# Seven block products in both feed-forward blocks, down sets 3 and 2 in turn

## The chip, the cores and the metric

One NeuronCore of a Trainium2 chip runs the whole program. The metric is the device time of one execution in microseconds. Engines as the profile names them: PE is TensorE, DVE VectorE, ACT ScalarE, POOL GpSimd, SP the engine that issues all DMAs here.

## The reference

Two transformer-like blocks on 1024 tokens of width 1024, all in float32. Only the feed-forward parts matter here:

```python
def swiglu(h, w_gate, w_up, w_down):                     # block 1, D_FF = 2816
    return (jax.nn.silu(h @ w_gate) * (h @ w_up)) @ w_down
...
h = h + swiglu(rmsnorm(h, norm_ffn[i]), w_gate[i], w_up[i], w_down[i])
...
h = rmsnorm_2(x, g_ffn[i])                               # block 2, D_FF_2 = 4096
x = x + jnp.square(jax.nn.relu(h @ w_ffn_up[i])) @ w_ffn_down[i]
```

## The kernel before

Each engine has one program, a chain of generators (`tensor`, `vector`, `scalar`, `gpsimd`, `sync`, L4056 to L4133), written out stage by stage: output projection of block 1 (`mix_`), FFN1 (`ffn_`), the latent projections (`z_`) and so on, `mix2_`, FFN2 (`ffn2_`), and a last gated stage (`ple_`). Every engine runs its list strictly in that order; semaphores (`Signal`) join them. A PSUM bank holds 128 x 512 floats; `tile_of` takes the next bank of a group and waits until its last tenant was read.

Precision: every operand is split into a high half (ScalarE copies into fp32r) and a low half (VectorE subtracts), and each product is three matmuls of 128 x 128 by 128 x 512: high by high, high by low, low by high.

FFN1 before (`ffn_blocks`, L1675 on) goes through the 22 row tiles of the hidden layer in chunks of 2 and then 4. For a pair of tiles it computes gate and up with `dense` (two tiles, two token halves, eight channel steps), multiplies by the norm's factor while draining (VectorE), applies Silu (ScalarE), multiplies, and splits the result into `f_hi` (ScalarE) and `f_lo` (POOL). Each chunk then has its down products, added to `hT` by VectorE. The weights stream through three slots of `wt1`. The last chunk's drains are followed tile by tile by the next stage's operand: ScalarE's high half and two squares, VectorE's low half and two sums (L1763 to L1771, L1823 to L1828).

FFN2 before uses seven block products in place of eight. A block of the up weights (8 channel tiles x 256 columns) and x are both seen as 2 x 2; `Sevens.add` makes four sums of quarters, `seven_products` runs seven products of depth 4 (84 matmuls) into three banks x, y, z in which the sums chain up (`BANK_OF`), ScalarE keeps the running bank three times (`kept`), and VectorE adds it to y and z. The first block is plain (96 matmuls), because the sums of x come late. VectorE also makes four differences of the f tiles, and SP stores seven tiles of 256 KB a block to `f_scratch`.

The down product (`Sets`, L565 on) has seven sets, each over all groups of depth 4, a piece being one set and group: 4 x 4 x 3 = 48 matmuls. Order 0, 3, 2, 6, 4, 1, 5. Weights and f come from DRAM, 1 MiB each a piece; a piece of sets 3, 2, 6 and 4 needs a sum of weights, made by VectorE in one of three `w_second` buffers. Set 3's sums are stored to DRAM and read by set 2, set 2's by set 6. Loads are issued four pieces ahead (`RINGS`), h is read back in quarters, and the set ends are added to it. SP's order in a piece is: wait for the piece, `second_free` (L627 to L631: the store that reads the buffer must have landed), loads, read-back, and the store of the sum two pieces on:

```python
        for i in range(LAST + 1):
            if i + RINGS <= LAST:
                q.wait_ge(*T.of("down2", i))
                dn.second_free(q, i + RINGS)
                dn.load_weights(q, i + RINGS)
                dn.load_moving(q, i + RINGS)
...
            if i + 2 <= LAST:
                dn.keep(q, i + 2)
```

## Time and profile before

| | us |
|---|---|
| median of 3 runs | 2906.4 (2905.8 to 2911.11) |
| the profiled execution | 2911.59 |
| its span, first to last instruction | 2909.8 |
| TensorE busy | 2765.3 (15516 matmuls) |
| VectorE, ScalarE, POOL busy | 1604.2, 864.7, 356.0 |
| FFN1 | 322.6 to 1050.1 |
| FFN2, up and down | 2110.0 to 2763.1 |

All times inside the execution are us from the start of its span. Matmuls overlap their neighbours, so busy times and lengths of one matmul say little; starts and the idle times before an instruction do. A number in square brackets behind a row is the idle time of that engine before it, with what ended it.

### The profile page before, as it was taken

To read this page: it belongs to the slowest core of one execution; us is meant where nothing else is said; L and a number is where in the kernel's file an instruction comes from. 1 tells how busy PE (TensorE), PEld (TensorE's weight loads), DVE (VectorE), ACT (ScalarE), POOL (GpSimd) and SP (SyncE) were. 2 spreads that over 40 slices of the span, in tenths; PEclk is the share of its full clock that TensorE was granted. 3 is DMA by queue.
4 is the path that set the end of the run, shared out by engine and by line. 5 is a ranking of instruction groups with operands and counts; after the bars stand their busy time and mean duration, and the time that the engine had idled before them with its cause. 6 is when DMAs were issued, how large, how long until landed. Compare 5 with 4: busy or idle time off the path is not lost.

```text
span 2909.8 us, 37491 instructions
## 1 busy us (share of the span) xinstructions
PE 2765.3 (95%) x15516; PEld 2238.0 (77%) x15516; DVE 1604.2 (55%) x2076; ACT 864.7 (30%) x1154; POOL 356.0 (12%) x326
## 2 busy tenths in 40 slices
PE   6889999999999999999989899989999999979998
PEld 5677878888888888887778667668888887768876
DVE  6995433232323354545554576655499886556464
ACT  4143312111111141114443443242343223324422
POOL 2000101000000101000000701203112221000021
PEclk9899999999999999999999999989999999999999
DMA  4051011111111112434556323434234447887411
GB/s 181 19 135 66 30 58 47 55 44 51 51 44 54 48 44 101 138 123 130 163 161 186 102 59 120 145 107 168 73 120 157 151 160 289 296 328 250 145 44 58
DMA packets 269384, 341.76 MB, mean 117 GB/s; under 512 B 63168, under 2 KB 177728, under 8 KB 266272
## 3 DMA queue, kind: packets, MB, share of 16 engines
q1 hardware_dynamic: 269216, 339.36, 35.1%
q8 instruction: 124, 2.03, 0.3%
q14 instruction: 44, 0.36, 0.0%
HBM read 241.41 MB, written 98.14 MB: 117 GB/s over the span
## 4 chain that ended last, share of the span: by engine, by line
PE 80%; DVE 8%; DMA 5%; ACT 2%; issue 2%; SPq 1%; POOL 1%; DVEq 0%; ACTq 0%; POOLq 0%
PE bank L858 14%; PE bank L859 13%; PE bank L860 13%; DMA w_sums_scratch<-w_second 4%; PE bank L884 3%; PE bank L885 3%; PE bank L887 3%; PE bank L3610 2%; PE bank L3612 2%; PE bank L3611 2%; PE bank L2086 2%; PE bank L2087 2%; PE bank L2088 2%; PE bank L2789 2%; PE bank L3046 1%
## 5 line engine op out<-in xcount | busy, mean ns | idle before, releaser
L858 PE MATMUL bank<-op_hi,w_hi 128*128 128x512 f32 x1312 | 513.7, 392 | 1.6 <-DVE gates L919 1.5
L860 PE MATMUL bank<-op_hi,w_lo 128*128 128x512 f32 x1312 | 512.0, 390 | 0.0
L859 PE MATMUL bank<-op_lo,w_hi 128*128 128x512 f32 x1312 | 511.9, 390 | 0.0
L183 DVE TENSOR_TENSOR w_lo<-w_raw,w_hi 128x2048 fp32r<-128x2048 f32 (+3 forms) x127 | 270.4, 2139 | 183.6 <-ACT w_hi L455 143.8
L858 PEld LDWEIGHTS bank<-op_hi,w_hi 128*128 128x128 f32 x1312 | 247.1, 188 | 53.4 <-issue 2.2
L859 PEld LDWEIGHTS bank<-op_lo,w_hi 128*128 128x128 f32 x1312 | 247.1, 188 | 51.4 <-issue 0.2
L860 PEld LDWEIGHTS bank<-op_hi,w_lo 128*128 128x128 f32 x1312 | 246.9, 188 | 51.5
L183 DVE TENSOR_TENSOR hT<-hT,bank 128x512 f32<-128x512 f32 x156 | 102.9, 685 | 189.5 <-PE bank L860 157.0
L455 ACT ACTIVATE w_hi<-w_raw 128x2048 fp32r<-128x2048 f32 (+2 forms) x83 | 141.5, 1710 | 217.6 <-DMA w_raw<-in_w_in 99.5
L3610 PE MATMUL bank<-w_hi,w_hi 128*128 128x512 f32 x448 | 177.7, 397 | 23.7 <-DVE w_lo L183 23.7
L183 POOL TENSOR_TENSOR sq_sum<-sq_sum,sq 128x1024 f32<-128x1024 f32 (+1 forms) x34 | 72.6, 2134 | 879.9 <-ACT sq L695 878.6
L3611 PE MATMUL bank<-w_lo,w_hi 128*128 128x512 f32 x448 | 176.9, 395 | 0.0
L3612 PE MATMUL bank<-w_hi,w_lo 128*128 128x512 f32 x448 | 176.8, 395 | 0.0
L884 PE MATMUL bank<-hi,hi 128*128 128x512 f32 x420 | 163.9, 390 | 2.0 <-DVE f_out L183 1.3
L183 POOL TENSOR_TENSOR f_lo<-h_tmp,f_hi 128x512 fp32r<-128x512 f32 x44 | 65.7, 1514 | 616.4 <-ACT f_hi L1753 616.4
L858 PE MATMUL bank<-f_hi,w_hi 128*128 128x512 f32 x352 | 137.7, 391 | 3.2 <-POOL f_lo L183 3.2
L859 PE MATMUL bank<-f_lo,w_hi 128*128 128x512 f32 x352 | 137.8, 391 | 0.0
L860 PE MATMUL bank<-f_hi,w_lo 128*128 128x512 f32 x352 | 137.7, 391 | 0.0
L183 DVE TENSOR_TENSOR h_tmp<-bank,rs 128x512 f32<-128x512 f32 x44 | 30.2, 686 | 171.2 <-PE bank L860 157.4
L3610 PEld LDWEIGHTS bank<-w_hi,w_hi 128*128 128x128 f32 x448 | 85.7, 191 | 44.7 <-DVE w_lo L183 26.9
L2086 PE MATMUL bank<-op_hi,w_hi 128*128 128x512 f32 x256 | 105.7, 413 | 1.7 <-DVE w_lo L183 1.7
L183 DVE TENSOR_TENSOR gates<-bank,rs 128x512 f32<-128x512 f32 x46 | 31.2, 691 | 133.9 <-PE bank L860 133.9
(516 smaller groups left out, 5409.3 us busy)
## 6 DMA issues: line engine op xcount, KB each, us to landing
f_scratch<-f_out SPq DMA_DIRECT2D x112, 256.0 KB, 2.0
w_raw<-f_scratch SPq DMA_DIRECT2D x28, 1024.0 KB, 9.6
w_raw<-in_w_ffn_down SPq DMA_DIRECT2D x24, 1024.0 KB, 5.4
record<-record_scratch SPq DMA_DIRECT2D x16, 1024.0 KB, 5.2
block<-in_w_ffn_up SPq DMA_DIRECT2D x16, 1024.0 KB, 5.3
w_raw<-in_w_in SPq DMA_DIRECT2D x13, 1024.0 KB, 5.7
w_second<-in_w_ffn_down SPq DMA_DIRECT2D x12, 1024.0 KB, 8.3
w_raw<-in_w_gate SPq DMA_DIRECT2D x11, 1024.0 KB, 5.2
```

The costliest lines, as they stand in the source:

```text
L183: return e.tensor_tensor(out, x, y, op)
L455: s.activation(self.flat(self.hi, i), self.flat(self.raw, i), ACT.Copy).then_inc(*self.hi_done.up(i))
L858: t.matmul(ps[:], hi[:, k, wc], x[0][:, k, xc], start=n == 0, stop=False)
L859: t.matmul(ps[:], hi[:, k, wc], x[1][:, (k + turn) % KD, xc], start=False, stop=False)
L860: last = t.matmul(ps[:], lo[:, k, wc], x[0][:, k, xc], start=False, stop=n == kt - 1)
L884: t.matmul(ps[:], w.hi(q, n)[:, j, :], x.hi(i, n)[:, j, :], start=start, stop=False, skip_group_check=more)
L885: t.matmul(ps[:], w.hi(q, n)[:, j, :], x.part(i, n, lo=1)[:, j, :], start=False, stop=False, skip_group_check=more)
L887: last = t.matmul(ps[:], w.part(q, n, lo=1)[:, j, :], x.hi(i, n)[:, j, :], start=False, stop=end, skip_group_check=more)
L2086: t.matmul(ps[:], hi[:, k, :], op[0][:, k, hs(half)], start=k == 0, stop=False)
L3610: t.matmul(ps[:], w[0][:, j, wc], x[0][:, j, :], start=start, stop=False, skip_group_check=more)
L3611: t.matmul(ps[:], w[0][:, j, wc], x[1][:, j, :], start=False, stop=False, skip_group_check=more)
L3612: last = t.matmul(ps[:], w[1][:, j, wc], x[0][:, j, :], start=False, stop=stop, skip_group_check=more)
```

## The change

FFN2's code becomes a class `Feed` with functions `first_scalar`, `first_vector`, `feed_sync`, `feed_tensor`, `feed_scalar`, `feed_vector` and `feed_gpsimd`, and FFN1 is run by the same functions. FFN1's blocks alternate between `w_gate` and `w_up` (22 blocks, the first plain); a gate block leaves its four tiles in `gate_ff` for Silu, an up block multiplies them in and makes the differences, with a single set of six f buffers. Its down product has 11 tiles of depth in groups of 4, 4 and 3, so 21 pieces, with three buffers of loads. h is stored before FFN1 and read back in its down part, as in FFN2. In `Sets`, in both blocks, sets 3 and 2 alternate group by group: the sum of set 2 is made from the sum of set 3 in the same buffer, and only the difference is stored for set 6. The finishing of the first four channels moves ahead of the end of the last piece in both blocks.

```diff
+        self.x_ff = self.sevens(HALF, 4, (98, 34, 46, 38, 54, 0, 58), [(18, (42, 62, 50))])
+        self.w_ff = self.sevens(P, 4, tuple(66 + n for n in range(7)),
+                                [(s, (s + 4, s + 5, s + 6)) for s in (82, 74, 4)])
+        self.gate_ff = [at(92 + i, "gate", [P, HALF]) for i in range(4)]
+        self.f_ff = [at(o, "f_out", [P, HALF]) for o in (14, 15, 81, 96, 97, 89)]
...
-    ORDER = (0, 3, 2, 6, 4, 1, 5)
-    WEIGHTS = {0: ((0, 0),), 3: ((0, 1), ALU.add, (1, 1)), 2: ("sum", ALU.subtract, (0, 0)),
+    ORDER = ((0,), (3, 2), (6,), (4,), (1,), (5,))
+    WEIGHTS = {0: ((0, 0),), 3: ((0, 1), ALU.add, (1, 1)), 2: ((0, 0), ALU.subtract, "sum"),
...
-        self.pieces = [(n, g) for n in self.ORDER for g in range(len(groups))]
-        self.sums = [i for i, (n, g) in enumerate(self.pieces) if len(self.WEIGHTS[n]) > 1]
-        self.saved = [i for i, (n, g) in enumerate(self.pieces) if n in self.KEPT]
+        self.pieces = [(n, g) for sets in self.ORDER for g in range(len(groups)) for n in sets]
+        self.sums = [i for i, (n, g) in enumerate(self.pieces) if n in (3, 6, 4)]
+        self.saved = [i for i, (n, g) in enumerate(self.pieces) if n == 2]
+
+    def second_of(self, i):
+        return i - 1 if i in self.saved else i
...
     def second_free(self, q, i):
         before = self.sums.index(i) - len(self.second) if i in self.sums else -1
         if before >= 0:
             j = self.sums[before]
-            q.wait_ge(*self.V.of(self.name, "w lo", j))
-            if j in self.saved:
-                q.wait_ge(*self.stores[self.saved.index(j) % 2].of(self.name, "kept", self.saved.index(j)))
+            if j + 1 in self.saved:
+                q.wait_ge(*self.V.of(self.name, "w lo", j + 1))
+                q.wait_ge(*self.kept(self.pieces[j][1]))
+            else:
+                q.wait_ge(*self.V.of(self.name, "w lo", j))
...
     def add(self, v, i):
-        if i in self.sums:
+        if self.summed(i):
             self.landed(v, i)
-            tt(v, self.other(i), self.flat(self.w[0], i), self.other(i), self.WEIGHTS[self.pieces[i][0]][1]).then_inc(
-                *self.adder.up(self.name, "sum", i))
+            x, y = self.flat(self.w[0], i), self.other(i)
+            if i in self.saved:
+                v.wait_ge(*self.A.of(self.name, "w hi", i - 1))
+                v.wait_ge(*self.V.of(self.name, "w lo", i - 1))
+                x, y = y, x
+            tt(v, self.other(i), x, y, self.WEIGHTS[self.pieces[i][0]][1]).then_inc(*self.adder.up(self.name, "sum", i))
...
+    def first_vector(v, F, residual):
...
+        for step in range(4):
+            if step == 3:
+                v.wait_ge(*F.x.summed(0, 0, 2))
+                for n in (0, 3, 6):
+                    F.x.plain_lo(v, 0, n, EARLY)
+            if F.free["sum"][step] is not None:
+                v.wait_ge(*T.of("op", F.free["sum"][step]))
+            F.x.add(v, 0, step, EARLY, spare=F.spare[0])
+        v.wait_ge(*F.x.summed(0))
+        F.x.plain_lo(v, 0, 1, EARLY)
+        yield from residual(6)
+        yield from residual(7)
...
+    def feed_sync(q, F, after_piece):
...
+        q.wait_ge(*T.of("up", F.last, 6))
+        dn.load_weights(q, 2)
+        q.wait_ge(*F.landing(7 * (F.pairs - 1)))
+        dn.load_moving(q, 2)
+        for m in range(1, 7):
+            store(F.last, m)
+        for m in range(7 * F.pairs - NG, 7 * F.pairs):
+            q.wait_ge(*F.landing(m))
+        q.wait_ge(*V.of("f sum", F.last, 6))
+        rings = len(dn.loaded)
+        for i in range(3, rings):
+            dn.load_weights(q, i)
+            dn.load_moving(q, i)
+        for i in range(F.LAST + 1):
+            if i + rings <= F.LAST:
+                q.wait_ge(*T.of("down", i))
+                dn.second_free(q, i + rings)
+                dn.load_weights(q, i + rings)
+                dn.load_moving(q, i + rings)
+            if i in F.back:
...
+            if i + 2 <= F.LAST:
+                dn.keep(q, i + 2)
+            after_piece(i)
+            yield
...
+        def silu(q, n):
+
+            if F.gate is None or F.makes_f(q) or n not in F_PIECES:
+                return
+            g = F.gate[F_PIECES[n]]
+            s.wait_ge(*(V.of("f sum", q, n) if n == 5 or q == 0 else G.of("f rs", q, n)))
+            s.activation(g, g, ACT.Silu).then_inc(*A.up("silu", F.pair(q), F_PIECES[n]))
...
+                if F.gate is None:
+                    stt(v, f, f, 0.0, f, ALU.max, ALU.mult).then_inc(*V.up("f", F.pair(q), e))
+                else:
+                    v.wait_ge(*A.of("silu", F.pair(q), e))
+                    tt(v, f, f, F.gate[e], ALU.mult).then_inc(*V.up("f", F.pair(q), e))
...
+    F1 = Feed("ff1", Sm, Sf, hT, nm1, "cols", "rs1", rs, 2 * (DFF // (2 * P)), ("w_gate", "w_up"), "w_down",
+              DFF // (2 * P), ((0, 4), (4, 4), (8, 3)), [x[:] for x in mem.gate_ff],
+              (mem.spare_ff, mem.kept_ff, [mem.f_ff]), mem.w_ff, mem.x_ff, (mem.w_sets1, mem.x_sets1, mem.w_second1),
+              d_seven[1:] + d_seven[:1], (0, 2, 5, 10),
+              dict(hi={1: 1, 6: 1, 3: 3}, sum=(3, None, 5, 5), late=lambda: wt1.used(B_OUT + 3), third=5))
...
     def ffn_tensor(t):
...
+        yield from feed_tensor(t, F1)
...
     def ffn_scalar(s):
...
+        def finished(k):
+            s.wait_ge(*Sf.V.of("acc", 1 if k < 4 else 5, k % 4))
+            s.activation(op[0][:, k, :], hT[:, k, :], ACT.Copy, scale=gg[:, k:k + 1]).then_inc(*A.up("hi", k))
+            nm_h.square(s, k, hT[:, k, :])
+            nm_x.square(s, k, hT[:, k, :], vec["norm_final"][:, k:k + 1])
+
+        def after_piece(i):
+            if i == LAST1 - 1:
+                s.wait_ge(*T.of("down", LAST1 - 1))
+                s.wait_ge(*Sf.V.of("gg"))
+                for k in range(4):
+                    finished(k)
+                wt1.split_hi(s, B_LAT)
+
+        yield from feed_scalar(s, F1, after_piece)
+        for k in range(4, KD):
+            finished(k)
...
     def ffn_vector(v):
...
+        def after_piece(i):
+            if i == 0:
+                tt(v, gg[:], vec["norm_final"], vec["g_mix_2"], ALU.mult).then_inc(*V.up("gg"))
+            if i == LAST1:
+                for k in range(4):
+                    finished(k)
+                wt1.split_lo(v, B_LAT)
+
+        yield from feed_vector(v, F1, after_piece, lambda p: finished(4 + p))
...
+    F2 = Feed("ff2", Sy, S2, hT2, nm_f, "cols y", "rs y", mem.rs_f, UP_PAIRS, ("w_ffn_up_2",), "w_ffn_down_2", UP_PAIRS,
+              tuple((4 * g, 4) for g in range(UP_PAIRS // 4)), None, (mem.x_spare, mem.kept_up, mem.f_out), mem.w_up,
+              mem.x_up, (mem.w_sets, mem.x_sets, mem.w_second), d_seven[1:] + d_seven[:1] + [d_xb], (0, 2, 6, 13),
+              dict(hi={6: 1, 3: 3}, sum=(1, 1, 3, 5), late=lambda: wt3.used(3), third=3))
```

## Rows read from the trace of the kernel before

**Rows 1.** The page's engine totals: busy us (share of the span) x instructions.

```profile
PE 2765.3 (95%) x15516; PEld 2238.0 (77%) x15516; DVE 1604.2 (55%) x2076; ACT 864.7 (30%) x1154; POOL 356.0 (12%) x326
```

**Rows 2.** Windows: length, busy us (x) of each engine, granted clock, DMA share, GB/s.

```profile
322.60:1050.10 727.50, 724.27 (x3200) 599.69 (x3199) 255.62 (x284) 140.35 (x147) 71.30 (x46) 1.00 0.15 48
...
2110.00:2426.30 316.30, 314.30 (x1397) 259.81 (x1395) 275.06 (x368) 104.28 (x168) 76.04 (x45) 0.99 0.43 150
...
2516.00:2610.00 94.00, 72.82 (x301) 57.95 (x300) 49.36 (x29) 22.30 (x12) 0.00 (x0) 0.95 0.86 313
```

**Rows 3.** TensorE's timeline: start us, length us, line, operands, count.

```profile
2110.03 0.39 PE L3570 MATMUL bank<-hi,hi 128*128 128x512 f32 x1
...
2128.84 0.39 PE L3572 MATMUL bank<-hi,block_lo 128*128 128x512 f32 x1
...
2132.73 0.77 PE L3570 MATMUL bank<-hi,hi 128*128 128x512 f32 x1
...
2135.84 0.40 PE L3571 MATMUL bank<-block_lo,hi 128*128 128x512 f32 x1
```

**Rows 4.** TensorE's waits: line <- releaser: us in total, times, longest us.

```profile
PE bank L3610 <- DVE w_lo L183: 23.7, 8, 7.7
...
PE bank L858 <- POOL f_lo L183: 3.2, 1, 3.2
```

**Rows 5.** VectorE's timeline before FFN2: quarter sums and low halves of x.

```profile
2102.61 5.09 DVE L183 TENSOR_TENSOR block_lo<-block,hi 128x1536 fp32r<-128x1536 f32 x3
...
2107.63 1.75 DVE L183 TENSOR_TENSOR sum<-block,sum 128x1536 f32<-128x1536 f32 x1
```

**Rows 6.** VectorE on the f tiles of FFN2: ns min/median/max.

```profile
L193 DVE SCALAR_TENSOR_TENSOR f_out<-f_out x64: 678/688/1790, 2146.8 to 2438.4; 128x512 f32<-128x512 f32 x64
```

**Rows 7.** Timeline in FFN2's down: SP's loads, VectorE's sums and low halves.

```profile
2444.15 0.38 SPq L608 DMA_DIRECT2D w_raw<-in_w_ffn_down  x1
...
2498.24 0.33 SPq L608 DMA_DIRECT2D w_raw<-w_sums_scratch  x1
...
2509.85 2.29 DVE L183 TENSOR_TENSOR w_second<-w_raw,w_second 128x2048 f32<-128x2048 f32 x1 [5.30 <-DMA w_raw<-f_scratch]
...
2516.46 2.28 DVE L183 TENSOR_TENSOR w_lo<-w_raw,w_hi 128x2048 fp32r<-128x2048 f32 x1
...
2654.45 0.37 SPq L608 DMA_DIRECT2D w_raw<-in_w_ffn_down  x1
...
2664.29 4.49 DVE L183 TENSOR_TENSOR w_lo<-w_raw,w_hi 128x2048 fp32r<-128x2048 f32 x2 [4.58 <-ACT w_hi L647]
```

**Rows 8.** A window of 10 us in FFN2's down, columns as in group 2.

```profile
2460.00:2470.00 10.00, 10.00 (x46) 8.29 (x45) 6.79 (x3) 3.72 (x2) 0.00 (x0) 1.00 1.05 409
```

**Rows 9.** Timeline at FFN1's end: ScalarE and VectorE for the next stage.

```profile
1018.25 1.15 ACT L1767 ACTIVATE op_hi<-hT,gg 128x1024 fp32r<-128x1024 f32 x1 [3.55 <-DVE hT L183]
...
1020.25 1.14 ACT L695 ACTIVATE gates<-hT,vec_cols 128x1024 f32<-128x1024 f32 x1
...
1044.03 1.28 DVE L193 SCALAR_TENSOR_TENSOR op_lo<-hT,gg,op_hi 128x1024 fp32r<-128x1024 f32 x1 [1.22 <-ACT op_hi L1767]
...
1045.23 1.22 DVE L183 TENSOR_TENSOR sq_sum<-sq_sum,sq 128x1024 f32<-128x1024 f32 x1
...
1063.80 1.90 ACT L455 ACTIVATE w_hi<-w_raw 128x2048 fp32r<-128x2048 f32 x1
...
1065.72 2.29 DVE L183 TENSOR_TENSOR w_lo<-w_raw,w_hi 128x2048 fp32r<-128x2048 f32 x1 [0.23 <-ACT w_hi L455]
```

**Rows 10.** A link of the chain of waits, and SP's waits, 2430 to 2765.

```profile
2530.30 15.30 DMA w_sums_scratch<-w_second
...
SPq L631 <- DMA w_sums_scratch<-w_second: 97.1, 8, 13.5
```

**Rows 11.** TensorE after the end of FFN2, waits of 0.3 us and more.

```profile
2765.28 0.47 PE L3887 MATMUL bank<-op_hi,w_hi 128*128 128x512 f32 x1 [2.07 <-DVE op_lo L193]
...
2778.69 0.47 PE L909 MATMUL bank<-ones,sq_sum 128*128 128x1 f32 x3 [2.24 <-POOL sq_sum L183]
```

More of the change, by code:

```diff
@@ L400, in wblock, with __init__ @@
     return (kt, cols, [(0, w[k0:k0 + kt * P, c0:c0 + cols].rearrange("(k p) c -> p k c", p=P))])
-def ffn_chunks(d_ff):
-    n_t = d_ff // P
-    first = n_t % FC or FC
-    return [(0, first)] + [(t0, FC) for t0 in range(first, n_t, FC)]
 class Weights:
-    def __init__(self, nc, name, tiles, plan, before=(), stage=None):
+    def __init__(self, nc, name, tiles, plan, before=(), stage=None, turn=None):
         self.name, self.plan, self.before = name, plan, before
@@ L1570, in mix_scalar @@
             yield
[L1571 removed]
+        for b in range(3):
             wt1.hi_at(s, B_OUT + b)
@@ new lines, in first_vector @@
+    def first_vector(v, F, residual):
+        A, T = F.before.A, F.before.T
+        for n in (0, 3, 1, 5):
+            F.w.plain_lo(v, 0, n, to=PLAIN_HI[n])
+        v.wait_ge(*A.of("scaled", 5))
+        v.wait_ge(*A.of(F.norm.name, "sq", 3))
+        v.wait_ge(*F.stored_out(3))
+        for step in range(4):
[10 more added lines that the diff above has]
+        yield from residual(7)
+        v.wait_ge(*A.of("scaled", 7))
+        v.wait_ge(*F.free["late"]())
+        for step in range(4):
+            F.x.add(v, 0, step, LATE, 1, F.spare[1])
+        v.wait_ge(*F.x.summed(0, 1))
+        for n in (0, 3, 1, 6):
+            F.x.plain_lo(v, 0, n, LATE, 1)
@@ L3597, in ffn2_tensor @@
-        for i, (n, g) in enumerate(dn.pieces):
-            w, x = dn.still(i), dn.through(i)
-            t.wait_ge(*V.of("down2", "w lo", i))
-            t.wait_ge(*V.of("down2", "x lo", i))
-            for p in range(4):
-                bank = ("down2", BANK_OF[n], p)
-                fresh = g == 0 and n in (0, 3, 1)
-                ps = tile_of(t, "low" if n == 0 else "high", *bank) if fresh else psum.tile(*bank)
-                if g == 0 and n in (2, 4, 5, 6):
-                    t.wait_ge(*V.of("acc", {2: 0, 4: 2, 5: 4, 6: 3}[n], p))
-                depth, wc = dn.depth(i), slice(p * P, p * P + P)
-                for j in range(depth):
-                    start, stop, more = fresh and j == 0, set_end(i) and j == depth - 1, n in (2, 4, 5, 6)
-                    t.matmul(ps[:], w[0][:, j, wc], x[0][:, j, :], start=start, stop=False, skip_group_check=more)
-                    t.matmul(ps[:], w[0][:, j, wc], x[1][:, j, :], start=False, stop=False, skip_group_check=more)
-                    last = t.matmul(ps[:], w[1][:, j, wc], x[0][:, j, :], start=False, stop=stop, skip_group_check=more)
-                if set_end(i):
-                    last.then_inc(*T.up("down2", "set", n, p))
-            if set_end(i):
-                T.also("down2", i)
-            else:
-                last.then_inc(*T.up("down2", i))
-            yield
```

1116 lines of the change are left out of this document (512 added, 604 removed).

## The prediction

> **What bounds the kernel now.** I read the page's engine totals first: TensorE is busy 2765.3 us of a span of 2909.8 [rows 1], so the time is the number of its matmuls, the pitch between them, and its pauses. The windows by stage come next [rows 2]: the first feed-forward block (FFN1, 322.6 to 1050.1) keeps TensorE busy throughout with VectorE at a third; the up products of the second (FFN2, 2110 to 2426) are also full, with VectorE at 275 of 316 us; and from 2516 to 2610 TensorE starts only 301 matmuls in 94 us. The 390 ns of a matmul on the page overlap its neighbours; the starts give the price: 2110.03 to 2128.84 holds 83 intervals, 0.2266 us each [rows 3]. The list of TensorE's waits is last [rows 4]: 23.7 us for the down product's low weight halves, one 3.2 us in FFN1.
>
> **1. FFN1 by seven products.** Before: 22 row tiles x 2 halves x 8 x 3 matmuls for gate and for up (2112) and 1056 for down, 3168 in all. After: one block of the 22 plain (96), 21 with 84, and down 7 x 11 x 4 x 3 = 924: 2784. 384 fewer x 0.2266 = **-87.0**. TensorE was full there, so all of it lies on the path, if the other engines keep up.
>
> **2. What goes with the old FFN1.** The wait for the low half of the first hidden tile, 3.2 us [rows 4]. A pause is followed by matmuls at half the granted clock, 2.4 to 1.2 GHz: after the small column sums of FFN2, the seven matmuls from 2132.73 to 2135.84 take 3.11 us instead of 1.59, so 1.5 us lost [rows 3]. Together **-4.9**.
>
> **3. Start of FFN1.** The column sums now take 32 small matmuls as in FFN2 instead of 16 (+1.5) and bring FFN2's half-clock spell (+1.5). The quarter sums need three quarters of x, each 1.75 us on VectorE, and four low halves, 1.70 us each ([rows 5], the same operations in FFN2). The last output block runs from 300.8 to 322.6 (96 matmuls back from [rows 2]). In FFN1 VectorE's first sum waits for its channel step 3 (311.7) and its third for step 5 (317.1), where FFN2 waits for steps 1 and 3. From 317.1 VectorE has two sums and four low halves, 10.4 us; TensorE needs the last of these for its second step at 325.3, and gets it at 327.5: **+2.2**. FFN1's rope work stays earlier, hidden by the output blocks.
>
> **4. Up products of FFN1.** A gate block adds on VectorE 4 sums, 7 low halves and 4 bank drains, an up block also 4 multiplications by the gate and 4 differences: 38 operations a pair, each near 0.69 as the shortest in [rows 6], 26.3 us, against 168 matmuls, 38.1 us. FFN2 puts 19 on every block of 19.0 us and TensorE hardly waited. Silu (4 a pair) has ScalarE's idle time; POOL's scaling keeps its place. The first pairs of FFN2 cost it some 1.5 us; I take **+1.5**, bounds 0 and 40 (below). The change up to down waits less than in FFN2 (there 2.6 us of the 23.7), since the block before the last makes no differences: **+0.3**.
>
> **5. Down of FFN1, three buffers deep.** A piece of depth 4 is 48 matmuls, 10.9 us; of depth 3, 8.2. The load of piece i+3 starts when piece i ends, so it has two pieces. Three MiB issued at 2498.24 were landed when VectorE's sum began at 2509.85, beside a store: 11.6 us; two MiB issued at 2654.45 gave the first low half at 2664.29, less ScalarE's 1.9 of high half: 7.9. I take 10.5 for three alone. From the sum's start to the end of the x low half is 2516.46 + 2.28 - 2509.85 = 8.9 [rows 7]. So 19.4 us from issue to ready. Against the windows:
> - Piece 3 (first summed one): SP must first issue the last f stores and wait for their landing; in FFN2 its next load is issued at 2444.15 [rows 7], 17.9 us after the up products' end [rows 2], which is 6.7 after the end of piece 0. Ready at 26.1, window 19.1: 7.0, plus a half-clock spell: +8.5.
> - Piece 9 (first of set 6): window two pieces of depth 3, 16.3 us; ready 19.8 with a small store beside it, and 0.7 for the add that frees its bank: +4.2, spell +1.5.
> - Pieces 12 and 13: window 19.1: +0.5 each.
> The others have 21.8 us or no sum. **+15.2**. Bounds: 0, if three MiB land at the full rate, 409 GB/s [rows 8]; 55, if every one of the 12 summed or chained pieces, and the others to a lesser part, loses what a piece loses at 2516 to 2610. I am nearest the middle rows, which are the same loads. The read-back of h (4 MiB) is queued behind the loads and has two pieces of slack.
>
> **6. End of FFN1.** ScalarE may write the new operand's first high half only when piece 19 has ended, one piece of depth 3 (8.2 us) before the end. It then has four channels, each a high half and two squares, 2.00 from first to third start plus 1.14 = 3.14 us, and only then the next weights' high half, 1.90: 14.5. VectorE's low half of those, 2.29, queued behind its sums of squares (1.22 each), ends at 17.1 [rows 9]; two drains of set 5 stand between it and the bank that the next stage opens first: 18.4. TensorE idles **10.2**. The column sums of the next stage need all eight channels; VectorE, with 3.7 us of work a channel (1.28 and two of 1.22, [rows 9]) and the last four drains, has them at 35.0, TensorE arrives at 31.9: **+3.1**; spell **+1.5**. Before, the same work lay inside the last down products, for which the matmuls of four tiles are longer. Bounds 8 and 20.
>
> FFN1: -87.0 - 4.9 + 3.0 + 2.2 + 1.5 + 0.3 + 15.2 + 14.8 = **-54.9**.
>
> **7. FFN2's down, sets 3 and 2 in turn.** In the chain of waits six links from 2499 to 2589 are stores of a weight sum, the one of the row 15.3 us long, and the next loads are issued only when each has landed; SP waits 97.1 us for these [rows 10]. A chained sum held its buffer until stored, and eight of sixteen were stored. Now set 2 makes its sum in the buffer of set 3, four are stored and four instead of eight read back, and three buffers last six pieces. Bytes per pair of pieces fall from 8 to 6 MiB, 289 GB/s, under the 409 of [rows 8]; VectorE's 17.8 of 21.8 us a pair fits; four buffers give a window of 32.7 us. 94 us less 301 x 0.2266 is 25.8, and the spell after 2610 1.2: **-27.0**, bounds -27 and -10 (some loads still behind a store).
>
> **8. End of FFN2.** Four of the eight channels are finished before the last piece ends, squares directly behind. The waits of 2.07 (2.2 with issue) and 2.24 (2.4) [rows 11] go: **-4.6**, bounds 0 and -6.
>
> **Sum**: -54.9 - 27.0 - 4.6 = -86.5. The profiled execution is 2911.6 us (span 2909.8 and 1.8 around it): 2825.1. The median of the runs is 5.2 lower: **2820**.
>
> **A rule weighed.** Rows of the down product move 409 GB/s from 2460 to 2470 [rows 8]. The Trainium skill, "DMA: Bandwidth & Descriptors", section Bandwidth, says that between HBM and SBUF a limit of about 358 GB/s per core binds. The trace does not agree here, with one core running. By that figure three MiB would land about 1.1 us later and FFN1's down would be some 5 us longer.
>
> **The rivals.**
> - (a) FFN1's down starves as FFN2's did: the two-piece window is missed by every summed piece. 12 x 3.4 (27.0 over the 8 pieces there) = 41 instead of 15: 2846. For it: one buffer less, and read-backs of h. Against: no load waits for a fresh store. Chance 0.15.
> - (b) The up products of FFN1 wait for the longer round through POOL's scaling, silu and the single f buffer: 2 us at each of 20 blocks, 2860. Against: two blocks lie between uses of each buffer. 0.08.
> - (c) The stalls of 5 and 6, 30.0 us, are covered but for 5: 2795. For it: three MiB at the rate of [rows 8] take 7.7 us, not 10.5. Against: the end of FFN1 is a chain of ScalarE work with no cover. 0.14.
> - (d) Slower than before: VectorE becomes the bound in FFN1's up products because its operations with two SBUF operands are stretched beside POOL. The longest such in FFN2 takes 1.79 against 0.69 [rows 6]. 30 a pair x 1.1 = 33 more, 59.3 against 38.1: 21 us x 10.5 pairs = +222, 3040. It decides from a stretch of 0.67 us on every one. Against: FFN2 had the same mix and denser. 0.02.
> - (e) FFN2's down keeps its pauses, since set 6 still reads stored sums and the loads bunch: 2843. 0.04.
>
> **How the numbers follow.** Forecast 0.57 (2806 to 2834). A measurement of this kernel tells 0.2% from no change. All cases but (d) are faster by far more: faster 0.97, same 0.01, slower 0.02. The range takes (c) and most of (a): 2795 to 2850, leaving out (b), (d) and the edges.
>
> **What would show it.** FFN1 from 322.6 to its last matmul near 985, matmul pitch 0.227; VectorE about 0.7 busy in its up products; pauses of TensorE near 7 and 4 us in the down part and one of about 10 before the latent products, each with a half-clock spell; in FFN2's down no wait of SP for a landed store before a load, and no pause over 1 us. Wrong if the up products show a pause in every block, or if the pauses in FFN1's down come at every piece.

## The result, and the profile after

| | before | after |
|---|---|---|
| median, us | 2906.57 (4 runs) | 2818.78 (4 runs, 2817.21 to 2821.49) |
| profiled execution, us | 2911.59 | 2817.73 |
| its span | 2909.8 | 2815.9 |

The ratio is 0.9696, with a 95% interval of 0.9679 to 0.9713: faster by 3.0%. The forecast was 2820, in a range of 2795 to 2850.

The engine totals on the page of the kernel after answer [rows 1]:

```profile
PE 2678.9 (95%) x15148; PEld 2166.8 (77%) x15148; DVE 1812.9 (64%) x2320; ACT 978.8 (35%) x1345; POOL 392.7 (14%) x344
```

TensorE's busy time fell by 86.4 us. VectorE has 209 us more to do and is not the bound. Windows of the kernel after, with the columns of [rows 2]: FFN1, FFN2's up products, and 94 us of FFN2's down product.

```profile
322.60:1019.00 696.40, 674.09 (x2954) 556.87 (x2953) 476.74 (x536) 260.73 (x340) 106.96 (x64) 0.97 0.43 148
2050.00:2366.50 316.50, 314.47 (x1398) 260.06 (x1397) 274.88 (x368) 104.31 (x168) 76.05 (x45) 0.99 0.43 150
2456.00:2550.00 94.00, 94.00 (x416) 77.85 (x415) 63.92 (x38) 29.88 (x17) 0.00 (x0) 1.00 0.87 319
```

The last row stands against 301 matmuls in as long a stretch before. In FFN1, TensorE now has what it did not have before: pauses, 22 us in its window. TensorE's timeline after, the rows with an idle time of 0.5 us or more in FFN1 (start, length, line, operands, idle time before):

```profile
328.58 0.68 PE L1893 MATMUL bank<-hi,hi 128*128 128x512 f32 x1 [2.03 <-DVE block_lo L183]
752.52 0.50 PE L887 MATMUL bank<-hi,hi 128*128 128x512 f32 x1 [0.69 <-ACT kept L1989]
760.74 0.47 PE L1933 MATMUL bank<-w_hi,w_hi 128*128 128x512 f32 x1 [2.48 <-DVE f_out L183]
793.38 0.47 PE L1933 MATMUL bank<-w_hi,w_hi 128*128 128x512 f32 x1 [0.84 <-DVE w_lo L183]
858.40 0.77 PE L1933 MATMUL bank<-w_hi,w_hi 128*128 128x512 f32 x1 [4.91 <-DVE hT L183]
890.54 0.47 PE L1933 MATMUL bank<-w_hi,w_hi 128*128 128x512 f32 x1 [0.60 <-DVE w_lo L183]
902.82 0.47 PE L1933 MATMUL bank<-w_hi,w_hi 128*128 128x512 f32 x1 [1.11 <-DVE w_lo L183]
991.63 0.77 PE L864 MATMUL bank<-op_hi,w_hi 128*128 128x512 f32 x1 [9.65 <-issue]
```

They lie where the prediction put them: the start (part 3), the change from up to down, pieces 3, 9, 12 and 13 (part 5), the end (part 6). Between 368 and 750 no up product waited. Behind some of them TensorE runs at half its clock for a while; such a spell is given below as the time that it loses against the full clock. In the last row nothing is named as releaser; the timeline of ScalarE and VectorE before it, also after, names the chain, and stands against [rows 9]:

```profile
973.86 1.15 ACT L2208 ACTIVATE op_hi<-hT,gg 128x1024 fp32r<-128x1024 f32 x1 [12.06 <-PE bank L1935]
...
985.99 1.89 ACT L456 ACTIVATE w_hi<-w_raw 128x2048 fp32r<-128x2048 f32 x1
...
988.05 2.29 DVE L183 TENSOR_TENSOR w_lo<-w_raw,w_hi 128x2048 fp32r<-128x2048 f32 x1
990.25 1.28 DVE L183 TENSOR_TENSOR hT<-hT,bank 128x512 f32<-128x512 f32 x2
...
1006.09 1.22 DVE L183 TENSOR_TENSOR gates<-gates,sq_x 128x1024 f32<-128x1024 f32 x1
```

ScalarE starts with piece 19's end (973.86), splits the next weights at 985.99, VectorE follows at 988.05, adds two banks of set 5 by 991.53, and TensorE starts at 991.63. SyncE's waits from 2300 to 2700, which stand against the 97.1 us of [rows 10]:

```profile
SPq L636 <- DMA w_sums_scratch<-w_second: 13.7, 2, 13.5
```

### The profile page after: what moved, and what is told of

Same layout as the page of the kernel before. It is cut to its first block, busy times and chain, and to the rows that moved or that the text cites. A ratio compares the mean times of both kernels' runs of the same rounds, so it can differ in the third digit from the quotient of the medians.

```text
span 2815.9 us, 37960 instructions
## 1 busy us (share of the span) xinstructions
PE 2678.9 (95%) x15148; PEld 2166.8 (77%) x15148; DVE 1812.9 (64%) x2320; ACT 978.8 (35%) x1345; POOL 392.7 (14%) x344
## 4 chain that ended last, share of the span: by engine, by line
PE 84%; DVE 9%; ACT 3%; issue 2%; DMA 2%; SPq 1%; POOL 0%; DVEq 0%; ACTq 0%; POOLq 0%
PE bank L887 8%; PE bank L888 8%; PE bank L890 8%; PE bank L864 6%; PE bank L866 6%; PE bank L865 6%; PE bank L1933 5%; PE bank L1934 5%; PE bank L1935 5%; PE bank L2500 2%; PE bank L2502 2%; PE bank L2501 2%; PE bank L3203 2%; DVE w_lo L183 1%; DMA w_raw<-f_scratch 1%
## 5 line engine op out<-in xcount | busy, mean ns | idle before, releaser
L887 PE MATMUL bank<-hi,hi 128*128 128x512 f32 x1008 | 392.8, 390 | 2.7 <-ACT kept L1989 1.4
L183 DVE TENSOR_TENSOR w_lo<-w_raw,w_hi 128x2048 fp32r<-128x2048 f32 (+3 forms) x123 | 256.0, 2096 | 154.9 <-ACT w_hi L456 86.4
L1933 PE MATMUL bank<-w_hi,w_hi 128*128 128x512 f32 x756 | 296.5, 392 | 12.5 <-DVE w_lo L183 5.1
L864 PE MATMUL bank<-op_hi,w_hi 128*128 128x512 f32 x608 | 239.9, 395 | 11.2 <-issue 9.6
L865 PE MATMUL bank<-op_lo,w_hi 128*128 128x512 f32 x608 | 238.3, 392 | 0.0
L866 PE MATMUL bank<-op_hi,w_lo 128*128 128x512 f32 x608 | 238.1, 392 | 0.0
L888 PE MATMUL bank<-block_lo,hi 128*128 128x512 f32 x576 | 224.1, 389 | 0.0
L890 PE MATMUL bank<-hi,block_lo 128*128 128x512 f32 x576 | 224.1, 389 | 0.0
L887 PEld LDWEIGHTS bank<-hi,hi 128*128 128x128 f32 x1008 | 189.4, 188 | 43.9 <-ACT kept L1989 2.2
L890 PE MATMUL bank<-hi,sum_lo 128*128 128x512 f32 x432 | 168.1, 389 | 0.0
L888 PE MATMUL bank<-sum_lo,hi 128*128 128x512 f32 x432 | 168.1, 389 | 0.0
L1934 PEld LDWEIGHTS bank<-w_lo,w_hi 128*128 128x128 f32 x756 | 143.0, 189 | 29.7
```

The costliest lines, as they stand in the source:

```text
L183: return e.tensor_tensor(out, x, y, op)
L864: t.matmul(ps[:], hi[:, k, wc], x[0][:, k, xc], start=n == 0, stop=False)
L865: t.matmul(ps[:], hi[:, k, wc], x[1][:, (k + turn) % KD, xc], start=False, stop=False)
L866: last = t.matmul(ps[:], lo[:, k, wc], x[0][:, k, xc], start=False, stop=n == kt - 1)
L887: t.matmul(ps[:], w.hi(q, n)[:, j, :], x.hi(i, n)[:, j, :], start=start, stop=False, skip_group_check=more)
L888: t.matmul(ps[:], w.hi(q, n)[:, j, :], x.part(i, n, lo=1)[:, j, :], start=False, stop=False, skip_group_check=more)
```

## The experiments

Times are medians. The runs of the kernel before beside them had medians of 2908.3, 2908.8 and 2908.4 in three groups, so a run is best set against the changed kernel, 2818.8 beside a kernel before of 2906.6. The changed kernel, run once more beside the last group, had 2819.9: a difference of 1 or 2 us between medians says nothing.

**The order of the sets alone.** The kernel before, with the class `Sets` of the changed one:

```diff
-    ORDER = (0, 3, 2, 6, 4, 1, 5)
+    ORDER = ((0,), (3, 2), (6,), (4,), (1,), (5,))
```

> The kernel before with one part of the change alone: the second block's down product takes sets 3 and 2 in turn, makes the sum of set 2 in the buffer of set 3 and stores four sums instead of eight; FFN1 stays as before. My theory (loads stood behind landings of stored sums): the 94 us stretch from 2516 to 2610 becomes a full one, 27 to 28 us less, 2879 us, and SyncE no longer waits for landed stores before loads; the end of FFN2, whose squares are not moved here, keeps its two waits and its spell. Rival 1 (the load rate was the limit, 8 MiB a pair of pieces against 6): only what the bytes give, a quarter of the 27, so about 2900. Rival 2 (the gain came with the new code at the end of FFN2 as well, the waits there being caused by the late down product): another 6 us less, 2873.

Measured: 2882.6 us (2881.4 to 2883.1), ratio 0.991 (0.9894 to 0.9927). The profiled executions differ by 28.7, the medians by 25.6. The window of [rows 2] in this kernel, and SyncE's waits from 2300 to 2700:

```profile
2516.00:2610.00 94.00, 94.00 (x416) 77.82 (x416) 64.41 (x38) 32.58 (x18) 0.00 (x0) 1.00 0.89 324
```

```profile
SPq L635 <- DMA w_sums_scratch<-w_second: 11.5, 2, 11.2
```

The same stretch goes from 301 matmuls to 416, and SyncE's wait for landed stores fell from 97.1 to 11.5 us. The total is 17 us below what rival 1 said. But the run changes two things at once, the waits and the bytes (6 MiB a pair of pieces instead of 8), and the rates of the stretch, 324 and 313 GB/s, don't part them: at an unchanged rate three quarters of the bytes would also give four thirds of the matmuls. The stretch before does better. Windows of the kernel before (the last two numbers are DMA share and GB/s):

```profile
2500.00:2512.00 12.00, 12.00 (x55) 9.94 (x54) 6.65 (x3) 1.76 (x1) 0.00 (x0) 1.00 0.96 338
2512.00:2516.00 4.00, 4.00 (x20) 3.30 (x19) 1.89 (x2) 3.72 (x2) 0.00 (x0) 1.00 0.30 72
```

The DMA engines ran out of work while SyncE stood at a store, and again from 2544 to 2548 (share 0.28) and from 2588 to 2592 (0.34). Over the 94 us the DMA share was 0.86 at 313 GB/s [rows 2]; my estimate from that is 364 GB/s at a full share, so 23.0 us for the 8 MiB of a pair, against TensorE's 21.8. Without the waits, the 8 MiB would have cost some 5 of the 25.8 us. So the waits are the larger part and the bytes a smaller one; no run has the one without the other. The two waits at FFN2's end stay as they were, 2.07 and 2.26 us (rival 2 falls).

**FFN1's end: the next weights split early.**

```diff
             if i == LAST1 - 1:
+                wt1.split_hi(s, B_LAT)
                 s.wait_ge(*T.of("down", LAST1 - 1))
...
-                wt1.split_hi(s, B_LAT)
...
+            if i == LAST1 - 1:
+                wt1.split_lo(v, B_LAT)
```

> The changed kernel, with ScalarE's high half and VectorE's low half of the first latent weight block made before the four finished channels instead of behind them. Theory A (as part 6 of the prediction: banks stand right behind the weights): the weights' 1.9 and 2.3 us leave the chain, but TensorE's first latent product then waits for two bank drains of set 5, which VectorE makes only after the low halves and sums of squares of channels 0 to 3, so the pause falls from 9.7 to about 7.4 and the total by 2 to 3 us, 2816.5. Theory B (the low half of the weights is the only thing late): TensorE starts right after the last down matmul, the pause goes and the kernel gains 9 to 10 us, 2809. Theory C (the column sums take its place, waiting for VectorE's sums of squares): gain 2 or less whatever the pause does.

Measured: 2815.6 us (2811.7 to 2815.9), 3.2 below the changed kernel. TensorE's first latent product in this kernel:

```profile
990.79 0.76 PE L864 MATMUL bank<-op_hi,w_hi 128*128 128x512 f32 x1 [7.44 <-issue]
```

9.65 became 7.44: theory A to 0.1 us. The weights were late by 2.2 us only; that the banks stood behind them is shown by a run below.

**FFN1's end: groups of depth 3, 4, 4.**

```diff
-              DFF // (2 * P), ((0, 4), (4, 4), (8, 3)), [x[:] for x in mem.gate_ff],
+              DFF // (2 * P), ((0, 3), (3, 4), (7, 4)), [x[:] for x in mem.gate_ff],
```

> The changed kernel with FFN1's down groups of depth 3, 4, 4 instead of 4, 4, 3. Window theory: the load of piece 9 then has pieces 7 and 8 of depth 4 before it, 21.8 us instead of 16.3, so the pause of 4.9 us at 858 and its spell of 1.3 go; the last piece is 2.7 us longer behind the point at which ScalarE may begin, so the pause before the latent products falls from 9.7 to about 7: together 8 to 9 us less, 2810. Rival (the load of piece 9 is late because of the small stores or of the read-back beside it, or the add that frees the bank is what TensorE waits for whatever the depth): piece 9 keeps 3 us or more, gain 3 to 5, 2815. Rival (the pause moves to another first piece of a set): no gain beyond the 2.7.

Measured: 2816.3 us (2811.0 to 2817.5), a gain of 2.5. The timeline of this kernel: the load of piece 5 by SyncE, VectorE's sum, TensorE's pause at piece 5 and the last one:

```profile
791.07 0.37 SPq L608 DMA_DIRECT2D w_raw<-in_w_down  x1
...
802.05 2.29 DVE L183 TENSOR_TENSOR w_second<-w_raw,w_second 128x2048 f32<-128x2048 f32 x1 [1.80 <-DMA w_raw<-f_scratch]
...
811.10 0.47 PE L1933 MATMUL bank<-w_hi,w_hi 128*128 128x512 f32 x1 [3.32 <-DVE w_lo L183]
...
986.52 0.76 PE L864 MATMUL bank<-op_hi,w_hi 128*128 128x512 f32 x1 [6.93 <-issue]
```

The pause of piece 9 is gone and the last one is 2.7 shorter, both as said. But piece 5 now waits 3.3 us and has a spell of 1.5. My window theory had looked at piece 9 alone. What both cases share: a piece of depth 4 behind two of depth 3 has 16.3 us for what takes 20 from issue to ready (791.07 to 810.95). Sets 3 and 2 in turn give two pieces of each group, so moving the short group moves such a piece from 9 to 5. The rival that the pause moves was right. The change from up to down got shorter as well, 1.42 us instead of 2.48 and without a spell (TensorE's wait at 760.85): piece 0 is of depth 3 here, and VectorE's two low halves of it take 4.5 us instead of 5.6.

**VectorE loaded in FFN1's up products.** Three of a weight block's four sums are repeated once; in a second run, three times (`range(3)`).

```diff
+        for _ in range(1 if self.name == "w_ff1" and i > 1 and step != 1 else 0):
+            tt(e, out, x, y, o).then_inc(*self.adder.up())
+            e.wait_ge(*self.adder.last())
         tt(e, out, x, y, o).then_inc(*self.adder.up(self.name, "sum", i, part, step))
```

> The changed kernel, with three of the four sums of every weight block in FFN1's up products made twice (same result, one more write of each): 3 more VectorE operations of 0.69 us in each of 20 blocks of 19 us, 2.1 us a block, some 42 us of VectorE work in all. Slack theory: VectorE has 5 us idle in a block (280 busy of 380), so TensorE's rows stay free of waits and the time is that of the changed kernel within 3 us, 2819 to 2822. Rival (the idle time is not usable, since the sums stand in the chain between banks and products): a wait at each block of 0.5 to 2 us, 2829 to 2860.

> As with three more sums a block, but nine more: three of the four weight sums made four times (same result), 6.2 us more VectorE work in each of FFN1's 20 blocks, 14 + 6.2 = 20.2 us for 19.0 of TensorE. Slack theory: VectorE becomes the bound of the up products, each block as long as its work: 20 x 1.2 = 24 us, with a half-clock spell where the pauses are long enough, so 25 to 50 us over the changed kernel, 2845 to 2870. Rival (the sums are made in a burst in front of the next bank sum, so each block has the full burst of 9 x 0.7 as a pause): 20 x 6 = 120, 2940. Rival (the work before was stretched by other engines and has room): no more than 10.

Measured: 2828.4 us (2825.1 to 2828.7) and 2907.1 us (2902.9 to 2910.1). The windows of the two in the up products, and TensorE's timeline in the second:

```profile
380.00:780.00 400.00, 396.56 (x1747) 327.84 (x1748) 326.09 (x441) 140.74 (x240) 103.31 (x62) 1.00 0.34 113
```

```profile
380.00:780.00 400.00, 354.57 (x1452) 285.24 (x1450) 347.18 (x486) 116.40 (x207) 85.20 (x51) 0.94 0.25 84
...
457.08 0.50 PE L890 MATMUL bank<-hi,hi 128*128 128x512 f32 x1 [2.85 <-DVE gate L183]
...
480.12 0.50 PE L890 MATMUL bank<-hi,hi 128*128 128x512 f32 x1 [2.08 <-DVE f_out L183]
...
502.35 0.50 PE L890 MATMUL bank<-hi,hi 128*128 128x512 f32 x1 [2.85 <-DVE gate L183]
```

With three more, the up products got two new waits, of 1.8 and 0.5 us, in the first pair, and no other: the slack is real. (The window's missing busy time is mostly the pause between up and down.) The median is 9.6 above the changed kernel, though, so the forecast of 2819 to 2822 missed, and the waits in the up products explain only 2.6 of it. By the two profiles, which differ by 10.9, 1.4 us lie before FFN1 and some 2.3 in its down part, where piece 3 waits 2.5 us instead of 0.8; the rest is spread over later stages whose work is the same. Those stages vary by as much in other profiles (see the changed kernel again, below), but this kernel's four runs all lie high, and why stays open. With nine more, two blocks take 45.3 us (457.08 to 502.35) instead of 38.1, and VectorE is 87% busy: 19.7 us a block. By work alone a block would be 0.7 us longer than TensorE's 19.0; it is 3.6 longer. So the price of the slack theory was too low (expected 25 to 50, measured 88), and the rival's too high (120). VectorE's timeline in this kernel, before TensorE's row of 480.12:

```profile
476.60 2.87 DVE L183 TENSOR_TENSOR sum<-block,sum 128x512 f32<-128x512 f32 x4
479.39 0.68 DVE L183 TENSOR_TENSOR f_out<-bank,kept 128x512 f32<-128x512 f32 x1
```

The sums stand in one burst, from 470.07 to 479.47, in front of the bank sum that TensorE waits for. That costs 2 to 4 us in every block and 6.4 in front of the first, with a half-clock spell behind 14 of the 20 pauses.

**From up to down: one low half moved up.** In both blocks, `split_lo` is cut into its two operations:

```diff
+            if (q, n) == (F.last, 4):
+                dn.split_w_lo(v, 0)
             if n in F_PIECES:
                 f_sum(q, n)
...
             if (q, n) == (F.last, 4):
-                dn.split_lo(v, 0)
+                dn.split_x_lo(v, 0)
```

> The changed kernel, with the low half of the first down weights (2.3 us of VectorE, in both blocks) made before the bank sum of the last block's product 4, where VectorE is idle (5.7 us in FFN1, 2.7 in FFN2), instead of behind it. Theory (the pause up to down, 2.6 us and 1.5 of spell, is the bank sum of product 6 queued behind both low halves of piece 0): in both blocks the pause falls below 0.8 and the spell goes. In FFN1 half of it is given back at piece 3, whose load SyncE cannot start earlier by more than the f pieces come earlier: 2 us there. Total 5 to 6 us less than the changed kernel, 2813. Rival (the pause is the 0.6 us copy and the sum themselves, a round through ScalarE and VectorE whatever the order): pause stays at 2 or more, total within 1 us.

Measured: 2817.4 us (2814.9 to 2818.0), only 1.4 below, which is hardly more than two groups of runs of one kernel differ by. FFN1's part of this kernel, from TensorE's, VectorE's and SyncE's timelines:

```profile
759.39 0.47 PE L1939 MATMUL bank<-w_hi,w_hi 128*128 128x512 f32 x1 [0.87 <-DVE f_out L183]
762.51 4.49 DVE L183 TENSOR_TENSOR w_lo<-w_raw,w_hi 128x2048 fp32r<-128x2048 f32 x2 [3.26 <-ACT w_hi L653]
773.94 0.38 SPq L608 DMA_DIRECT2D w_raw<-in_w_down  x1
794.02 0.77 PE L1939 MATMUL bank<-w_hi,w_hi 128*128 128x512 f32 x1 [4.44 <-DVE w_lo L183]
```

The cause of the pause is shown: 2.48 became 0.87, and in FFN2 0.36, with no spell in either. In the changed kernel the two low halves were in front of it as one stretch:

```profile
753.38 1.67 POOL L183 TENSOR_TENSOR f_out<-f_out,rs 128x512 f32<-128x512 f32 x1 [5.29 <-DVE f_out L183]
753.81 5.59 DVE L183 TENSOR_TENSOR w_lo<-w_raw,w_hi 128x2048 fp32r<-128x2048 f32 x2
```

The first of the two takes 3.4 us where every later one of its size in FFN1's down takes 2.3: POOL scales an f tile beside it. So 1.1 us of the stretch is what rival (d) of the prediction had in mind, at this one place. FFN2, four buffers deep, kept the gain (3.7 us). FFN1 gained 3.1 at the change and paid 7.4 at piece 3 (4.6, spell 2.8) where it had paid 1.0: the load of piece 3 was issued at 773.94, as late as before, while TensorE was earlier. I had expected half to be given back.

**And the last f pieces moved up too**, on top of the edit above, in FFN1:

```diff
-        dn.split_lo(v, 1)
         for n in (4, 5, 6):
             f_end(F.last, n)
         f_differences(F.last, range(4))
+        dn.split_lo(v, 1)
```

> The kernel of the low half moved up, with one more edit in FFN1: the last f pieces (three multiplications by the gate, four differences) are made before the low halves of piece 1, not behind them. Theory (piece 3 gave the gain back because its load, three buffers deep, stands on SyncE's queue behind the last f stores, which wait for VectorE, which waits for the landing of piece 1's moving operand): the six stores and then the load of piece 3 are issued by the end of piece 0, near 771 instead of 773.9, and the pause at piece 3 falls from 4.4 and 2.8 of spell to 1.5 or less; about 5 less than the run with the low half alone, 2812. Rival 1 (the load waits for the landing of those stores or for the rate, 3 MiB in 10.8 us): issue stays near 773 and the pause at 4. Rival 2 (the low halves of piece 1 now come late and TensorE waits there): a new pause of 1 to 3 at piece 1, 2815.

Measured: 2814.4 us (2805.5 to 2818.0). In this kernel:

```profile
771.50 0.38 SPq L608 DMA_DIRECT2D w_raw<-in_w_down  x1
...
791.51 0.47 PE L1939 MATMUL bank<-w_hi,w_hi 128*128 128x512 f32 x1 [1.06 <-DVE w_lo L183]
```

The load goes out at piece 0's end and the pause is 1.06, with no spell; no new pause stands at piece 1. So the f pieces behind the low halves of piece 1 held the load: the chain was the landing of piece 1's operand, VectorE's low halves of it, the f pieces behind them, SyncE's stores behind those, and the load of piece 3 last. The median gained 3 of the expected 5; its runs are the widest of all (12.5 us), and the profiled one is the lowest, 9 us under the median. So the timeline carries the verdict on the pause, and the gain in the total is not shown beyond these 3 us.

**FFN1's end in full.** Groups of 3, 4, 4, the early weights, and two banks of set 5 added between the low halves of channels 1 to 3:

```diff
             if i == LAST1:
                 for k in range(4):
                     finished(k)
+                    if k in (1, 2):
+                        F1.bank_add(5, k - 1)
```

> The changed kernel with three edits at FFN1's end: groups of depth 3, 4, 4; the first latent weights split before the finished channels; and VectorE adds the first two banks of set 5 between the low halves of channels 1 to 3 instead of behind all sums of squares. Chain theory: the pause before the latent products (9.7 us) goes down to below 1, as the two banks and the weights were what it waited for, and in its place TensorE waits some 5 to 7 us at the column sums, for VectorE's 3.7 us a channel: the column sums start 20 to 22 us after the last down matmul instead of 26.6. The end of FFN1 gains about 5, the pause of piece 9 goes, and one of 3 comes at piece 5 as in the run with the groups alone: 2811. Rival (whatever holds the latent products is something else, the high or low half of channel 0 or the next weights): the pause stays at 4 or more.

Measured: 2808.6 us (2808.2 to 2814.4). TensorE's first latent product and first column sum in this kernel:

```profile
979.26 0.47 PE L864 MATMUL bank<-op_hi,w_hi 128*128 128x512 f32 x1 [0.66 <-issue]
...
996.65 0.35 PE L2208 MATMUL bank<-ones,sq_sum 128*128 128x1 f32 x2 [3.51 <-DVE sq_sum L183]
```

The idle time of 9.65 fell to 0.66, where the run with the groups alone took 2.7 off it and the one with the weights alone 2.2: weights and banks were all that it waited for. The column sums took its place with 3.5 us (expected 5 to 7) and begin 18.4 us after the last down matmul instead of 26.6.

**All edits**, the last one excepted, and the column sums one channel from the end of their block:

```diff
-        norm = ({5: lambda: norm_h_tensor(t), 7: lambda: spread_tensor(t, Sf.T, ncol[:, 2, :], "rs2", Sf.V.of("rs2_col"))},
+        norm = ({7: lambda: norm_h_tensor(t)},
...
+            if b == 0:
+                spread_tensor(t, Sf.T, ncol[:, 2, :], "rs2", Sf.V.of("rs2_col"))
```

> All edits together: the three at FFN1's end, the low half of the first down weights moved up in both blocks, and the column sums of the latent stage one channel from its end (before channel 7 instead of before channel 5), the spread of the result behind the block. Theory: the column sums are reached 19 us after the last down matmul, when VectorE is nearly ready (20 to 22), so 2 us of pause instead of 6: FFN1's end 10 us shorter than in the changed kernel, up to down 6 us, piece 9 about 2: 2802. Rival (what is gained at the column sums is lost behind them, since the scale of the latent products comes later and their banks are drained later): 2808 to 2811.

> All edits and the last f pieces before the low halves of piece 1. Theory (with groups of 3, 4, 4 the pause stands at piece 5, whose load is issued at the end of piece 2 and has only two pieces of depth 3, 16.3 us, in front of it, whatever came before): piece 5 keeps 3.5 to 4.7 us and its spell, the gain is 0.5 or none, 2801. Rival (the pause at piece 5 is an echo of late stores and loads): it goes, 2796.

Measured: 2801.8 us (2798.2 to 2805.6), ratio to the kernel before 0.9635 (0.9621 to 0.965), 17 us below the changed kernel: the fastest of this study, where 2802 was expected. The timeline of TensorE in it, the first column sum and the next wait behind it:

```profile
1000.46 0.28 PE L2216 MATMUL bank<-ones,sq_sum 128*128 128x1 f32 x2
...
1018.83 0.47 PE L870 MATMUL bank<-op_hi,w_hi 128*128 128x512 f32 x1 [0.99 <-ACT rs L933]
```

The column sums no longer wait, and 1.0 us is left at the scale of the latent products. Piece 5 waits 4.5 us here (at 812.38), with a spell. With the f pieces moved up too it is 2804.8 (2799.0 to 2808.9), which can't be told from it. The rows of the two pauses in the last kernel:

```profile
765.23 0.47 PE L1939 MATMUL bank<-w_hi,w_hi 128*128 128x512 f32 x1 [1.79 <-DVE w_lo L183]
...
807.18 0.47 PE L1939 MATMUL bank<-w_hi,w_hi 128*128 128x512 f32 x1 [3.59 <-DVE w_lo L183]
```

Piece 5 keeps 3.6 of its 4.5 us, as two short pieces before it say, this time without a spell; so at most 0.9 of it was an echo of late stores. Piece 1 now waits 1.8, the second rival of the run before.

**The changed kernel again.**

> The changed kernel as it is, beside the others on the same chip: 2817 to 2821, and in the profile pauses of the same places within 0.5 us. What differs between its two profiled executions is the uncertainty of every term that the comparison of two profiles gives.

Measured: 2819.9 us (2817.3 to 2823.1). Two rows of its timeline:

```profile
854.34 0.77 PE L1933 MATMUL bank<-w_hi,w_hi 128*128 128x512 f32 x1 [5.02 <-DVE hT L183]
...
988.42 0.77 PE L864 MATMUL bank<-op_hi,w_hi 128*128 128x512 f32 x1 [9.66 <-issue]
```

Pauses agree within 0.4 us. Half-clock spells don't: the one after piece 9's pause cost 1.3 us in the first profile and 2.7 in this, the one after FFN1's column sums 2.4 and 1.6, and the one after the first pause of FFN1 (2.03 us in both) 1.9 and nothing. The stages between the two blocks differ more. From TensorE's wait of 1.53 us behind the first latent block to its first wait in FFN2's up products, 1053.74 to 2099.08 in the changed kernel, the same 7452 matmuls run in all thirteen profiles, and in the eleven of the changed kernel and its variants the code is the same too. This part took from 1042.4 us (the f pieces moved up too) to 1049.3 (groups of 3, 4, 4); in the two profiles of the changed kernel it took 1045.3 and 1049.0. A difference of two profiles is good to some 2 us in FFN1, and to no better than 7 in the long middle, so only the pauses read at their own place decide anything.

## Why the prediction was right, and where it was not

The total was 1.2 us off, and that is luck: it is closer than the working deserves. By profiled executions the sum was to be -86.5 and was -93.9; but the profiled run of before lay 5.0 us over its median and that of after 1.1 under, so the medians moved by 87.8. Two things cancelled, the stalls of FFN1 that were taken too dear and the place of the two profiles beside their medians.

| term, us | predicted | measured in the profiles |
|---|---|---|
| 2 old waits of FFN1 | -4.9 | gone |
| 3 start, column sums and low half | +5.2 | pause 2.0, spells 1.9 and 2.4 with the sums |
| 4 up products | +1.5 | 1.0 |
| 4 up to down | +0.3 | 2.6 and spell 1.5 |
| 5 piece 3 | +8.5 | 1.0 |
| 5 piece 9 | +5.7 | 5.1 and spell 1.3 |
| 5 pieces 12 and 13 | +1.0 | 2.0 |
| 6 pause at the end | +10.2 | 9.7 |
| 6 column sums, spell | +3.1, +1.5 | 0, 2.9 |
| FFN1 with the 384 matmuls | -54.9 | -58 |
| 7 FFN2's down | -27.0 | -27.8 |
| 8 FFN2's end | -4.6 | -6.1, with the spell behind it |
| between the two blocks | 0 | -1.7 |

**What held, and by which run.** Part 1, the largest term, rests on the count: 368 fewer records of matmuls (384 less 16 more column sums), at an unchanged pitch, in up products without a wait. Part 7 is the one term tested alone: 28.7 us by the profiles, 25.6 by the medians, 27.7 from the first down product to the first product behind FFN2 (2429.06 to 2765.28 before, 2428.23 to 2736.80 in that run). It went through the waits for landed stores for the most part. What the change holds beyond it, FFN1 and FFN2's end, is the distance between that run and the changed kernel, 63.8 us, where -54.9 and -4.6 were forecast. Part 6's chain was right link by link: taking the weights out left 7.4, taking the banks out as well left 0.7. Part 4's slack held in the up products with three more operations a block, though not in the total. Piece 9's window was right in kind, 0.9 short in size (a pause of 4.2 forecast, 5.1 measured), and the run with another group order showed the same at the one other piece that came to stand behind two short ones. Of the rivals, (a), (b), (c) and (e) are ruled out by the timeline after ((e)'s 2843 should have been 2847 by part 7's own 27.0). So is (d), VectorE as the bound, since no up product waited; its price would have needed far more work, for even at 19.7 us a block the loss is 88 us, not 222.

**Mis-sized: up to down, +0.3 against 4.1.** I argued from what would be missing in FFN1 (the differences of the last block but one). What made the pause was another thing, the bank sum of product 6 queued behind two low halves (5.6 us together in FFN1, 4.5 in FFN2), and that is the same in both blocks. Moving one low half showed it.

**Mis-sized: piece 3, +8.5 against 1.0.** I took SyncE's 17.9 us from FFN2 as if it stood against an undelayed piece 0. Here the load was issued 15.5 us after the last up product (773.60), and piece 0 itself ended 4 us late because of the pause that I had missed. The two errors are one: with that pause removed, piece 3 cost 7.4. Together the terms were +8.8 and came to 5.1. The run that moved the f pieces too shows what was held by the stores: without them the load goes out at piece 0's end and the pause is 1.06.

**Mis-sized: column sums, +3.1 against 0.** VectorE was ready at 1007.3, 1.5 us before my 35.0 from the chain's start (973.86). TensorE came at 1008.23, 34.4 from that start where I had 31.9, since its first fourteen matmuls after the pause ran at half the clock; I had added that spell to the total and not to TensorE's arrival. The price was real behind it: once the pause was gone, 3.5 us stood there.

**Mis-sized: FFN2's end, -4.6 against -6.1.** I counted the two waits and not the spell of 1.5 us behind the second, which went with them.

**Left open:** the 1.7 us between the two blocks, within the 7 us by which these same stages vary, and some 5 us of the run with three more sums. That seven products save FFN1 their whole 87.0 us has no run of its own; it follows from the count of matmuls and the pitch.

**The rule that was weighed.** The trace after says the same as [rows 8] did: the Trainium skill, "DMA: Bandwidth & Descriptors", section Bandwidth, puts about 358 GB/s per core as the limit, and the loads of FFN1's down product moved 389 GB/s with one core running. A note of the same section gives the 358 for both cores of the HBM domain streaming, which no run here does. The note fits the trace, and the rule as I had weighed it does not. Its window:

```profile
776.00:786.00 10.00, 10.00 (x45) 8.28 (x45) 1.63 (x1) 0.00 (x0) 0.00 (x0) 1.00 1.03 389
```

## What to carry to other kernels

A pause that you remove upstream is worth only what the next transfer can follow: where buffers are three deep, look up who issues the next load and what stands before it on its queue, and move that first. With pieces of uneven size, check every piece against the two before it, not the one that is late now. And at a join of two stages, list all that the first instruction waits for with the time of each; the gain of removing one is the distance to the next, which here was foretold to 0.1 us.

## What the runs showed of the hardware

After an idle time of 2 to 10 us TensorE mostly runs at the lower of its two clocks for a while, 1.2 instead of 2.4 GHz. Its timeline after the pause at FFN1's end, in the changed kernel, starts 0.43 us apart instead of 0.23, and the granted clock of 992 to 998 is 0.52 of the full one:

```profile
992.20 0.63 PE L865 MATMUL bank<-op_lo,w_hi 128*128 128x512 f32 x1
992.62 0.63 PE L866 MATMUL bank<-op_hi,w_lo 128*128 128x512 f32 x1
...
997.98 0.39 PE L864 MATMUL bank<-op_hi,w_hi 128*128 128x512 f32 x1
998.21 0.40 PE L865 MATMUL bank<-op_lo,w_hi 128*128 128x512 f32 x1
```

```profile
992.00:998.00 6.00, 6.00 (x16) 4.62 (x16) 5.85 (x6) 6.00 (x7) 0.00 (x0) 0.52 0.00 0
```

The spell costs 1.3 to 2.9 us in FFN1 and varies between two executions of one kernel by a factor of two, or is there in one and missing in the other. After some pauses of 3.3 to 3.6 us it came (at 811.10 with groups of 3, 4, 4), after others not (at 807.18 in the kernel with all edits and the f pieces). Over all thirteen profiles, matmuls of 512 columns stand behind 97 pauses of 0.45 to 1.2 us, and none has a spell; behind pauses of 1.6 to 2.3 us 17 of 65 have one, behind 2.3 to 3.0 us 40 of 49, behind 3.0 to 3.7 us 19 of 22, and behind longer ones all 34.

A run of one-column matmuls lowers the clock as well, with no pause before it. The column sums of the latent stage are 64 records of such matmuls, two to a row here, from 1008.23 to 1018.84 in the changed kernel. The rows start 0.22 us apart at first and 0.43 from 1011.58 on, and the granted clock of 1012 to 1018 is 0.50:

```profile
1010.82 0.36 PE L2199 MATMUL bank<-ones,sq_sum 128*128 128x1 f32 x2
...
1012.44 0.56 PE L2199 MATMUL bank<-ones,sq_x 128*128 128x1 f32 x2
1012.86 0.56 PE L2199 MATMUL bank<-ones,gates 128*128 128x1 f32 x2
```

```profile
1012.00:1018.00 6.00, 6.00 (x30) 6.00 (x30) 0.00 (x0) 0.00 (x0) 0.00 (x0) 0.50 0.00 0
```

The kernel before does the same in the same sums (from 1067.5), so this is no cost of the change. In the fastest kernel, whose last pause before the sums is one of 0.66 us, 19 us before them, the clock falls in them too (from 1003.4).

A store can hold a queue for long: a stored sum of weights, 1 MiB beside the loads, took 12.1 to 15.3 us from issue to landing in the kernel before, and each wait of SyncE for one kept all loads behind it from being issued.
